# Three-term split FFN on one core: gate products of seven of eleven rounds by a seven-product scheme

## What is computed

```python
SEQ, D_MODEL, FFN_DIM = 512, 1024, 2816
for i in range(2):                       # first block
    ...
    h = rms_norm(x, norm_ffn_pre[i])
    ff = (jax.nn.silu(h @ w_ffn_gate[i]) * (h @ w_ffn_up[i])) @ w_ffn_down[i]
    x = x + rms_norm(ff, norm_ffn_post[i])
    ...
...                                      # second block
    return (jax.nn.gelu(g) * val) @ w_down
```

## Time and profile before

| | |
|---|---|
| median of 3 runs | 2928.62 us (2928.1 to 2929.34) |
| the profiled execution | 2927.99 us |
| its span in the profile | 2926.2 us |
| TensorE (PE) busy | 99%, 14888 matmuls |
| weight loads of TensorE (PEld), beside the matmuls | 82% |
| VectorE (DVE), ScalarE (ACT), GpSimd (POOL) busy | 53%, 46%, 49% |
| granted TensorE clock, all 40 slices | 1.0 of full speed |
| weights loaded | 502 units of 512 KB, 94 GB/s over the span |

### The profile page before, as it was taken

How to read it: one execution, slowest core, us unless ns; L and a number is a source line. 1 busy time by engine, 2 the same in 40 slices (tenths; PEclk the granted TensorE clock), 3 DMA queues, 4 the chain that set the end, 5 groups by cost and what they waited for, 6 DMA issues and landing times. The chain is left out here.

```text
span 2926.2 us, 40035 instructions
## 1 busy us (share of the span) xinstructions
PE 2906.4 (99%) x14888; PEld 2405.1 (82%) x14888; DVE 1545.5 (53%) x2476; ACT 1342.3 (46%) x2089; POOL 1426.2 (49%) x825
## 2 busy tenths in 40 slices
PE   9999999999999999999999999999999999999999
PEld 7888888888878888888888877778888887888888
DVE  5657534221053667434222076655767688476766
ACT  4556545232243556445222255554444447443443
POOL 4454355444444554355444444344647462456655
PEclk9999999999999999999999999999999999999999
DMA  4222232233322222233233322113323222223322
GB/s 145 74 87 80 80 122 94 93 100 101 102 93 87 73 94 66 94 116 105 94 100 101 103 85 79 59 44 101 101 94 101 94 97 92 93 94 108 102 94 101
DMA packets 77305, 273.78 MB, mean 94 GB/s; under 512 B 8776, under 2 KB 9416, under 8 KB 77152
## 3 DMA queue, kind: packets, MB, share of 16 engines
q1 hardware_dynamic: 74112, 266.05, 27.6%
q10 hardware_dynamic: 3040, 5.64, 0.6%
HBM read 269.55 MB, written 2.10 MB: 93 GB/s over the span
## 5 line engine op out<-in xcount | busy, mean ns | idle before, releaser
L3238 POOL TENSOR_TENSOR WLO<-WRAW,WHI 128x1024 fp32r<-128x1024 f32 x355 | 859.3, 2424 | 1006.3 <-ACT WHI L1704 1003.4
L934 PE MATMUL ps<-HH,WHI 128*128 128x512 f32 x2144 | 842.2, 393 | 3.1 <-POOL WLO L3238 1.3
L936 PE MATMUL ps<-HH,WLO 128*128 128x512 f32 x2144 | 834.8, 389 | 0.0
L935 PE MATMUL ps<-HL,WHI 128*128 128x512 f32 x2144 | 834.5, 389 | 0.0
L1704 ACT ACTIVATE WHI<-WRAW 128x1024 fp32r<-128x1024 f32 x435 | 457.2, 1052 | 154.2 <-DMA WRAW<-wall 154.2
L934 PEld LDWEIGHTS ps<-HH,WHI 128*128 128x128 f32 x2144 | 402.6, 188 | 92.2 <-issue 5.3
L936 PEld LDWEIGHTS ps<-HH,WLO 128*128 128x128 f32 x2144 | 402.5, 188 | 84.5
L935 PEld LDWEIGHTS ps<-HL,WHI 128*128 128x128 f32 x2144 | 402.8, 188 | 80.7
L2463 DVE TENSOR_TENSOR ACC<-ACC,SQ 128x512 f32<-128x512 f32 x78 | 70.6, 906 | 281.3 <-ACT SQ L2000 271.1
L2981 DVE SCALAR_TENSOR_TENSOR ps<-U,COLS,ps 128x512 f32<-128x512 f32 x192 | 145.1, 756 | 85.2 <-ACT ps L2174 81.8
L3348 POOL TENSOR_SCALAR SG<-SG,RS 128x512 f32<-128x512 f32 (+3 forms) x104 | 110.1, 1069 | 140.4 <-DVE RS L2743 140.4
(11 more groups left out here) (460 smaller groups left out, 5749.0 us busy)
## 6 DMA issues: line engine op xcount, KB each, us to landing
WRAW<-wall SPq DMA_DIRECT2D x502, 512.0 KB, 3.3
y<-X ACTq DMA_DIRECT2D x8, 256.0 KB, 2.1
X<-xin SPq DMA_DIRECT2D x3, 512.0 KB, 7.7
DFT<-dft ACTq DMA_DIRECT2D x4, 258.0 KB, 4.1
PT_IN<-pin ACTq DMA_DIRECT2D x2, 512.0 KB, 3.6
DIL<-dil ACTq DMA_DIRECT2D x1, 768.0 KB, 4.4
X<-xin SPq DMA_DIRECT2D x2, 256.0 KB, 4.6
COLS<-cols ACTq DMA_DIRECT2D x1, 290.5 KB, 5.3
```

The source lines that it names most:

```text
L934: pe.matmul(out_, WHI[w_at], x_hi, start=first, stop=False)
L935: pe.matmul(out_, WHI[w_at], x_lo, start=False, stop=False)
L936: return pe.matmul(out_, WLO[w_at], x_hi, start=False, stop=last)
L3238: pool.tensor_tensor(WLO[:, s, :], whole, WHI[:, s, :].bitcast(F32), ALU.subtract).then_inc(wt_lo, 1)
```

## The change

For rounds 1 to 7 of each layer's swiglu (tiles 2 to 15) the gate products are made as in the paired stages: a round has now two plain up units and two paired gate units, which hold four quadrants of the gate weights of two tiles. The stage is cut in three: an "opened" swiglu stage with the round 0 alone, the new `swiglu_pairs` with seven rounds, and a swiglu stage with the last three.

- In a paired round the up units come first; the paired units add up in banks 4 to 7. At the end of a round ScalarE copies a half bank (`first_copied`), VectorE adds the seven half banks up and scales them with `RBX` in seven steps (`gates_added`, `pair_step`), ScalarE applies Silu twice, VectorE multiplies twice into `FR`.
- The mixed rows are made once a layer, for four pairs kp of row tiles: ScalarE makes scaled copies of the rows (`rows_gained`, eight activations), VectorE the three steps of T1 to T4 (`rows_mixed`), ScalarE rounds them to `HMH` (`mixed_hi`), VectorE makes `HML` (`rows_low`). TensorE waits for pair k in the first paired round, ahead of the product m = 2 of each step of depth (k = 2b + i), that is the third and the sixth product of a unit.
- Both units of the first paired round have all their sums made by GpSimd; in the others VectorE makes the first unit's, GpSimd the second's. The sums have EXTRA_1 = 3 places here.
- The rounding of the 16 products of rounds 0 to 7, from `FR` to `F1H` and `F1L`, is moved into the first two of the last three rounds.
- In the last `down` of each convolutional FFN VectorE finishes tile 1 at step 5 instead of step 3.
- The swiglu stages are written out, without loops; SyncE's loop is shorter, and 422 loads are written out instead of 150. The number of units is the same.

```diff
-EXTRA = 4
+EXTRA, EXTRA_1 = 4, 3
+GATE_ROUNDS = 7
+KEPT_TILES = 2 + 2 * GATE_ROUNDS
...
+            if 2 <= n < KEPT_TILES:
+                for m in range(2):
+                    product("w_ffn_up", l, DM, (n + m) * P)
+                for b in range(2):
+                    u.append(("w_ffn_gate paired", l, 2 * b, 2, n * P, 2 * P))
+                continue
+            for m in range(2):
+                product("w_ffn_gate", l, DM, (n + m) * P)
+                product("w_ffn_up", l, DM, (n + m) * P)
...
+    if t != 2 and n in GATES:
+        return {"pool": FORMS, "vector": ()} if k else {"pool": (), "vector": FORMS}
...
-        add("swiglu", FT1 // 2, 4, 4, {"gate_ready": 2, "product_ready": 2, "operand_hi_ready": 2, "operand_ready": 2}, op=op, norm=n).op_hi = op_hi
-        op = need(FT1)
+        opened = add("swiglu", 1, 4, 4, {"gate_ready": 2, "product_ready": 2}, op=op, norm=n, gain=f"norm_ffn_pre{l}")
+        opened.op_hi = op_hi
+        gates = add("swiglu_pairs", 1, 4 * GATE_ROUNDS, 2 * GATE_ROUNDS,
+                    {"rows_gained": 4, "mixed": 12, "mixed_hi_ready": 4, "mixed_ready": 4, "first_copied": GATE_ROUNDS, "pair_step": PAIR_STEPS * GATE_ROUNDS,
+                     "gate_ready": 2 * GATE_ROUNDS, "product_ready": 2 * GATE_ROUNDS, "kept_hi_ready": KEPT_TILES, "kept_ready": KEPT_TILES}, made=opened)
+        opened.pairs = gates
+        left = (FT1 - KEPT_TILES) // 2
+        add("swiglu", left, 4, 4, {"gate_ready": 2, "product_ready": 2, "operand_hi_ready": 2, "operand_ready": 2}, t=KEPT_TILES).kept = gates
...
-            return {3: (0, 1), 4: (), 5: (2, 3)}.get(j, tiles_done(st, j - 1))
+            return {3: (0,), 4: (), 5: (1, 2, 3)}.get(j, tiles_done(st, j - 1))
...
+            def swiglu_pairs(st):
+                for r in range(GATE_ROUNDS):
+                    for j in range(2):
+                        tile(st, 4 * r + j, 2 * r + j, 0, pair["H"], DT)
+                    for b in range(2):
+                        u = st.unit(4 * r + 2 + b)
+                        s, xlo, xhi = u % SLOTS, extras(u)[1], extras(u)[2]
+                        if b == 0 and r:
+                            pe.wait_ge(S["pair_step"], st.at("pair_step", PAIR_STEPS * r))
+                        if b == 0 and r == 0:
+                            pe.wait_ge(S["factor_rows_ready"], st.at("factor_rows_ready", 0))
+                        pe.wait_ge(slot_lo, PAIRED[u] + 1)
+                        for i, m in SLOTS_FIRST:
+                            h, home, block_, x = PRODUCTS[m]
+                            k = 2 * b + i
+                            if r == 0 and m == 2:
+                                pe.wait_ge(S["mixed_ready"], st.at("mixed_ready", k + 1))
+                            if (i, m) == (0, 3):
+                                weights(u)
+                            at = slice((2 * block_ + i) * P, (2 * block_ + i + 1) * P)
+                            w_hi, w_lo = (WHI[:, s, at], WLO[:, s, at]) if home == "slot" else (xhi[:, at], xlo[:, at])
+                            x_hi, x_lo = (HH, HL) if x < T1 else (HMH, HML)
+                            row, cols_ = 2 * k + x % 4 // 2, slice(x % 2 * HALF, (x % 2 + 1) * HALF)
+                            o = ps[4 + h // 2][:, h % 2 * HALF:(h % 2 + 1) * HALF]
+                            first = k == 0 and h in (0, 2, 4, 6)
+                            last = k == 3 and h in (1, 3, 5, 6)
+                            pe.matmul(o, w_hi, x_hi[:, row, cols_], start=first, stop=False, skip_group_check=True)
+                            pe.matmul(o, w_hi, x_lo[:, row, cols_], start=False, stop=False, skip_group_check=True)
+                            mm = pe.matmul(o, w_lo, x_hi[:, row, cols_], start=False, stop=last, skip_group_check=True)
+                            if (i, m) == (1, 2):
+                                mm.then_inc(slot_used, 1)
+                        mm.then_inc(unit_used, 1)
...
+            def rows_gained(st, kp):
+                if kp >= 2:
+                    act.wait_ge(S["mixed"], st.at("mixed", 3 * (kp - 2) + 3))
+                x = gained(kp)
+                for m in range(2):
+                    ins = act.activation(x[:, m, :], X[:, 2 * kp + m, :], ACT.Copy, scale=col(st.made.gain, 2 * kp + m))
+                ins.then_inc(S["rows_gained"], 1)
+            def mixed_hi(st, kp):
+                act.wait_ge(S["mixed"], st.at("mixed", 3 * kp + 3))
+                act.activation(HMH[:, 2 * kp:2 * kp + 2, :], mixed_at(kp), ACT.Copy).then_inc(S["mixed_hi_ready"], 1)
...
+            def swiglu_pairs(st):
+                mixed_hi(st, 0)
+                rows_gained(st, 2)
+                mixed_hi(st, 1)
+                rows_gained(st, 3)
+                for kp in range(2, 4):
+                    mixed_hi(st, kp)
+                for r in range(GATE_ROUNDS):
+                    for j in range(4):
+                        prepared(st, 4 * r + j)
...
+            def rows_mixed(st, kp):
+                b, t = halves(gained(kp)), halves(mixed_at(kp))
+                dve.wait_ge(S["rows_gained"], st.at("rows_gained", kp + 1))
+                if kp >= 2:
+                    dve.wait_ge(S["mixed_ready"], st.at("mixed_ready", kp - 1))
+                dve.tensor_tensor(t[:, 0:2, :], b[:, 1:2, :].to_broadcast([P, 2, HALF]), b[:, 0:4:3, :], ALU.subtract).then_inc(S["mixed"], 1)
+                dve.wait_ge(S["mixed"], st.at("mixed", 3 * kp + 1))
+                dve.tensor_tensor(t[:, 2, :], t[:, 1, :], b[:, 0, :], ALU.subtract).then_inc(S["mixed"], 1)
+                dve.wait_ge(S["mixed"], st.at("mixed", 3 * kp + 2))
+                dve.tensor_tensor(t[:, 3, :], b[:, 2, :], t[:, 2, :], ALU.add).then_inc(S["mixed"], 1)
+            def rows_low(st, kp):
+                dve.wait_ge(S["mixed_hi_ready"], st.at("mixed_hi_ready", kp + 1))
+                at = slice(2 * kp, 2 * kp + 2)
+                dve.tensor_tensor(HML[:, at, :], mixed_at(kp), HMH[:, at, :].bitcast(F32), ALU.subtract).then_inc(S["mixed_ready"], 1)
...
                             scaled(st, j, r, SG[:, k, :])
+                            if st.pairs is not None and j == 2:
+                                rows_mixed(st.pairs, 0)
+                                rows_mixed(st.pairs, 1)
...
+            def swiglu_pairs(st):
+                rows_low(st, 0)
+                rows_mixed(st, 2)
+                rows_low(st, 1)
+                rows_mixed(st, 3)
+                rows_low(st, 2)
+                rows_low(st, 3)
+                for r in range(GATE_ROUNDS):
+                    sums_of(st, 4 * r)
+                    for m in range(2):
+                        dve.wait_ge(unit_used, st.unit(4 * r + m) + 1)
+                        if r:
+                            dve.wait_ge(S["product_ready"], st.at("product_ready", 2 * r - 1 + m))
+                        scaled(st, 2 * r + m, 0, SG[:, 2 + m, :])
+                    if r == 0:
+                        dve.wait_ge(S["mixed_ready"], st.at("mixed_ready", 4))
+                    sums_of(st, 4 * r + 3)
+                    gates_added(st, r)
+                    for m in range(2):
+                        dve.wait_ge(S["gate_ready"], st.at("gate_ready", 2 * r + m + 1))
+                        dve.wait_ge(bank_free[st.bank(2 * r + m)], st.use(2 * r + m) + 1)
+                        dve.tensor_tensor(FR[:, 2 + 2 * r + m, :], SG[:, 2 + m, :], SG[:, m, :], ALU.mult).then_inc(S["product_ready"], 1)
+            def gates_added(st, r):
+                n = 0
+                def step(ins):
+                    nonlocal n
+                    ins.then_inc(S["pair_step"], 1)
+                    n += 1
+                def wait(k):
+                    dve.wait_ge(S["pair_step"], st.at("pair_step", PAIR_STEPS * r + k))
+                t = halves(TM)
+                both = ps[6][:, :].rearrange("p (n c) -> p n c", c=HALF)
+                dve.wait_ge(S["first_copied"], st.at("first_copied", r + 1))
+                step(dve.tensor_tensor(t[:, 3, :], t[:, 0, :], ps[4][:, HALF:SEQ], ALU.add))
+                wait(1)
+                step(dve.tensor_tensor(t[:, 1, :], t[:, 3, :], ps[6][:, HALF:SEQ], ALU.subtract))
+                step(dve.tensor_tensor(t[:, 2, :], t[:, 3, :], ps[7][:, 0:HALF], ALU.subtract))
+                wait(2)
+                step(dve.tensor_tensor(ps[5][:, :], ps[5][:, :], TM[:, 0, :], ALU.add))
+                wait(3)
+                step(dve.tensor_tensor(both, both, t[:, 2:3, :].to_broadcast([P, 2, HALF]), ALU.subtract))
+                wait(4)
+                step(dve.tensor_tensor(SG[:, 0, :], ps[5][:, :], RBX[:, :], ALU.mult))
+                wait(5)
+                step(dve.tensor_tensor(SG[:, 1, :], ps[6][:, :], RBX[:, :], ALU.mult))
```

More of the change, by code:

```diff
@@ L867, in sums_free, with extras, gained, mixed_at @@
         def sums_free(engine, n):
-            if PAIRED[n] >= EXTRA:
-                engine.wait_ge(unit_used, PAIRED_UNITS[PAIRED[n] - EXTRA] + 1)
```

(9 more changed lines are left out.)

105 lines of the change are left out of this document (75 added, 30 removed).

## The result

The changed kernel takes 2943.96 us (median of 5, 2942.38 to 2944.76), the one before in the same session 2928.74 (2928.1 to 2933.59): a ratio of 1.0048, 95% interval 1.0034 to 1.0062. It is 15.2 us slower; 7.9 were forecast. The profiled execution took 2943.96 us, with a span of 2942.1 where before it was 2926.2, 15.9 more.

The account below looks back on a forecast made before the run. TensorE, busy 99% of the span, was taken as the bound. Terms -11.2 - 0.9 + 19.2 + 0.9 = +8.0 on the profiled 2927.99 gave 2936.0, with the median 0.63 above it 2936.5 us; range 2919 to 2945.

Parts of the forecast that it names:

- A: The forecast case: the opening's mixing chain loses 7 to 12 us a layer, total 2931 to 2942 us; chance 0.55.
- D: More waits: half-bank adding or GpSimd late every round, or the clock falls in gaps; 2942 to 2960 us, chance 0.12.
- the prediction's own sign: Wrong if first paired rounds' waits sum under 7 or over 12 us a layer; also expected PEclk 1.0.
- Term 1: TensorE's stream in paired rounds: 20.96 us a round instead of 21.76, over 2 x 7 rounds -11.2 us.
- The estimate from the Trainium skill: TensorE's stream by the formula N/2.4 + 2.5 ns a matmul: 16.6 us saved, forecast 5.4 us lower.
- Term 3 and the restarts: First paired round: TensorE stalls for late mixed rows and remainders, +19.2 us; slower first matmuls after 8 waits, +0.9 us.
- The dates of `HML` and `WLO`: Layer 0's opening: `HML` of pair 0 at 496.3, of pair 1 at 500.3, second unit's 768-wide remainder at 506.05 us.
- Rival C: Opening: mixing done before TensorE's third product, a layer loses 1 us, total 2918.6 us; chance 0.16.
- Term 2: End of the first convolutional FFN: finishing tile 1 later removes TensorE's 0.92 us wait for half banks, -0.9 us.
- The bound that I gave, +5.8: End of the first convolutional FFN: upper bound if tile 1's two operations came on the path at 2.89 us each.
- A term at nothing, the moved rounding: Two later swiglu rounds: 8 x 0.63 us on ScalarE and 8 x 0.69 on VectorE each, fitting beside 22 us, no cost.
- The other terms at nothing: The six other paired rounds, with GpSimd busy 16.3 of 20.96 us, and the written-out loads cost nothing.

Follow-up runs that it names:

- run 5: Changed kernel with filler matmuls of a constant ahead of TensorE's first two waits for mixed rows in each layer: 2944.5 us.
- run 3: Changed kernel with two plain rounds ahead of six paired ones, the mixing of rows spread over the plain ones: 2933.56 us.
- run 1: Changed kernel with tile 1 finished at step 3 again, ScalarE's list at step 5 whole again: 2938.64 us.
- run 4: Changed kernel with the rounding of kept products moved behind each step's scaling and weight copy, on ScalarE and VectorE: 2940.89 us.
- runs 9 and 10: The 2919.8 us kernel with sums all by GpSimd from the third paired round, or all by VectorE from the second: 2919.53 and 2919.31 us.
- runs 6 and 8: Changed kernel with two plain rounds first, later rounding, old finishing, weight copies before mixing: 2925.48 us; then also before round 1's Silus, last `HMH` before `XHI`: 2919.8 us.

## Why the prediction was right, and which steps failed

The sign was right and the time lies in the range, and the sum was 7.3 us too low. The case was A's only in part. The time is above A's 2931 to 2942, in the band given to D (2942 to 2960), but not by what D named: no round is late, and the fall of the clock cost next to nothing in the opening, where D had it. Each layer's opening lost 8.6 and 9.0 us, inside A's 7 to 12; by the prediction's own sign, though, it was wrong there, since the waits alone sum to 5.2 and 4.8 us, under its 7, and PEclk is not 1.0. That the whole stayed in the range, 1 us below its upper end, is partly luck: two terms came out 9.3 us dearer than forecast, and one 2.5 us cheaper. By its terms:

- **Term 1, -11.2: right.** 20.98 us a round against 20.96. The estimate from the Trainium skill ("TensorE: Matmul & The Clock Gate", section "Back-to-back issue gap"), 16.6 us saved, was the worse one: its formula, which the page gives for a matmul by itself, was 11 ns too short for each in this stream; the pitch of the trace before held.
- **Term 3 and the restarts, +20.1: right in mechanism, 2.5 too high.** The openings cost 8.6 and 9.0. The dates of `HML` and `WLO` came within 1.2 us of the forecast, in part because errors cancelled: the scaling of round 0's last tile (0.68 us) was left out ahead of its product, while the mixing of pair 1 ended 0.7 us earlier than reckoned, and pair 1's `HML`, reckoned beside two operations of GpSimd's, was made while GpSimd stood idle. The waits alone are 5.2 and 4.8 us (forecast 9.6 with the clock at full speed); most of the rest went into slow matmuls, and run 5 shows that these change nothing there. Rival D had the fall of the clock, priced at up to 4.3 us a layer; its price in the opening is 0.1 us at most, since the next waits took it up, as D's sentence had allowed. That gaps drop the clock to half (the Trainium skill, "TensorE: Matmul & The Clock Gate", section "HAM oscillation — how this bites in real kernels"), which no row of before could show, this trace shows with 0.53 granted from 2407 to 2411 us, behind a wait of 3.07. The exclusion of VectorE and GpSimd that the chain rests on ("SBUF — State Buffer" of the Trainium skill, section "SBUF: two separate sides") is borne out by run 3: 0.42 alone, 2.45 beside a remainder. Rival C (chance 0.16) needed pair 1's last two steps ahead of GpSimd's first remainder; they took 1.96 and 2.50 us beside the remainders, and C did not come.
- **Term 2, -0.9: wrong, measured +5.9 in the trace and 5.3 by run 1.** The step that failed is "what is late next is tile 1 itself, but tiles 2 and 3 are finished at that later step already". I had rows of 2.38 and 2.89 us for the moved operations in hand and put them at nothing, since the tiles there had taken 0.7 us each. But the later place has its own release behind it, the next adding and the sum of squares, and the two operations met GpSimd's remainders there as well. The bound that I gave, +5.8, was what happened, by another way: 3.07 us of wait and 3.3 us of slow clock, less the 0.92.
- **A term at nothing, the moved rounding: wrong, +3.1 by run 4.** I compared busy sums with the room in a round (5.5 + 5.5 of 22 us) and not the place in the queue, and I took 0.69 us for a subtraction that takes 1.5 beside GpSimd. Both mistakes are one: a sum of busy times says nothing of what stands behind the moved work on its engine.
- **The other terms at nothing: right.** The steady rounds have no wait, in runs 9 and 10 not even with all sums on one engine. No wait of TensorE's is released by a load, so the written-out loads cost nothing that shows. (Each paired unit whose sums GpSimd makes has six instructions there, four sums and two remainders, as in the forecast's 16.3 us, and not seven.)

Together: -11.2 + 17.6 + 3.1 + 5.3 = +14.8, against 15.2 between the medians.

## What to carry to other kernels

Price a moved operation at its new neighbours, not at its duration alone: find what is queued behind it on its own engine, and which engine waits for that. A chain that opens a cheaper scheme can eat what many cheap rounds give (17.6 us against 11.2); spread it over work that has room, and put the copies that feed the weights' pipeline ahead of it: runs 6 and 8 differ in that order on ScalarE alone and lie 5.7 us apart, 4.3 by the kernel before beside each. A granted clock below 1.0 was a cost only where no later wait took it up: the same fall cost at most 0.1 us in the opening, and 3.3 us behind the sum of squares.
